# Output projection taken third by third, with all eight weight pieces resident and each third's norm behind its last step

## The reference

```python
def merge_and_mlp(h, ret_o, fox_o, ga, gb, w_ret_out, w_fox_out, w_o, norm2_g, w_ff1, w_ff2):
    m = jax.nn.sigmoid(ga) * (ret_o @ w_ret_out) + jax.nn.sigmoid(gb) * (fox_o @ w_fox_out)
    h = h + m @ w_o
    u = jax.nn.relu(rmsnorm(h, norm2_g) @ w_ff1)
    return h + (u * u) @ w_ff2
```

## Time and profile before

| what | us |
|---|---|
| median of 3 runs | 2191.03 |
| lowest and highest of them | 2190.86, 2191.83 |
| the profiled execution, its own time | 2192.57 |
| its span, first to last instruction | 2190.9 |
| PE busy in it | 2140.1 (98%) |
| DVE busy | 1066.9 (49%) |
| ACT busy | 543.5 (25%) |
| mean granted clock of TensorE | 0.995 of full speed |

### The profile page before, as it was taken

The page is one execution under the profiler, slowest core; times in us unless marked ns, Lnnn a source line. Parts: engine busy times, 40 slices in busy tenths (PEclk is TensorE's granted clock), DMA queues, the critical chain, the costliest instruction groups (busy, mean ns, idle before and its releaser), DMA issues.

```text
span 2190.9 us, 31673 instructions
## 1 busy us (share of the span) xinstructions
PE 2140.1 (98%) x12659; PEld 2002.2 (91%) x12659; DVE 1066.9 (49%) x2183; ACT 543.5 (25%) x1108; POOL 49.9 (2%) x93
## 2 busy tenths in 40 slices
PE   5999999999999999999999999999999999999998
PEld 4878888889998899989989999999999999999998
DVE  5354522256666666665665635574333333333333
ACT  4423200022222222221132323231212212122130
POOL 0000000000000000000000000000000000000000
PEclk9999999999999999999999999999999999999999
DMA  4222232433232333246434542012111111111111
GB/s 140 81 81 79 79 119 79 143 113 99 87 120 68 124 123 104 90 133 220 134 120 149 172 149 68 20 39 65 42 49 48 39 49 48 47 41 48 49 39 80
DMA packets 186189, 195.93 MB, mean 89 GB/s; under 512 B 9480, under 2 KB 156616, under 8 KB 186064
## 3 DMA queue, kind: packets, MB, share of 16 engines
q1 hardware_dynamic: 173904, 149.37, 22.3%
q0 software_dynamic: 12160, 44.72, 5.4%
HBM read 145.02 MB, written 49.04 MB: 89 GB/s over the span
## 4 chain that ended last, share of the span: by engine, by line
PE 92%; DVE 4%; issue 1%; ACT 1%; DMA 1%; DVEq 0%; SPq 0%; ACTq 0%
PE ps_mlp L303 37%; PE ps_dense L303 24%; PE ps_dense L324 18%; PE ps_out L928 4%; PE ps_scores L897 3%; PE ps_turn L881 2%; DVE w_lo L290 1%; PE ps_scores L973 1%; PE ps_turn L874 1%; PE ps_scores L979 1%; PE ps_scores L978 1%; DVE act_lo L364 0%; PE ps_turn L879 0%; DVE hn_T L1783 0%; PE ps_turn L1010 0%
## 5 line engine op out<-in xcount | busy, mean ns | idle before, releaser
L303 PE MATMUL ps_dense<-act_hi,w_lo 128*128 128x352 f32 (+2 forms) x1152 | 386.6, 336 | 0.6 <-DVE gated L1648 0.6
L303 PE MATMUL ps_dense<-act_hi,w_hi 128*128 128x352 f32 (+2 forms) x1152 | 384.8, 334 | 0.0
L303 PE MATMUL ps_dense<-act_lo,w_hi 128*128 128x352 f32 (+2 forms) x1152 | 384.7, 334 | 0.0
L303 PE MATMUL ps_mlp<-act_hi,w_lo 128*128 128x352 f32 x960 | 312.7, 326 | 3.5 <-DVE act_lo L1775 3.4
L303 PE MATMUL ps_mlp<-act_lo,w_hi 128*128 128x352 f32 x960 | 310.5, 323 | 0.0
L303 PE MATMUL ps_mlp<-act_hi,w_hi 128*128 128x352 f32 x960 | 310.1, 323 | 0.0
L279 ACT CAST w_hi<-w_raw 128x1024 fp32r<-128x1024 f32 x132 | 137.4, 1045 | 458.0 <-PE ps_mlp L303 283.8
L303 PE MATMUL ps_mlp<-u_lo,w_hi 128*128 128x352 f32 x768 | 248.0, 323 | 0.0
L303 PE MATMUL ps_mlp<-u_hi,w_lo 128*128 128x352 f32 x768 | 247.7, 323 | 0.0
L303 PE MATMUL ps_mlp<-u_hi,w_hi 128*128 128x352 f32 x768 | 247.6, 322 | 0.0
L303 PEld LDWEIGHTS ps_dense<-act_hi,w_hi 128*128 128x128 f32 x1152 | 218.0, 189 | 4.8 <-issue 1.6
(11 more groups left out here) (256 smaller groups left out, 2952.8 us busy)
## 6 DMA issues: line engine op xcount, KB each, us to landing
w_raw<-in_w_in SPq DMA_DIRECT2D x65, 512.0 KB, 4.3
w_raw<-in_w_ff SPq DMA_DIRECT2D x64, 512.0 KB, 3.9
gates<-stage POOLq DMA_DIRECT2D x24, 528.0 KB, 3.8
stage<-gates SPq DMA_DIRECT2D x16, 528.0 KB, 3.7
negc_rows<-neg_cumsum SPq DMA_DIRECT2D x8, 792.0 KB, 7.5
rotated<-stage POOLq DMA_DIRECT2D x8, 536.0 KB, 3.0
fox_out_T<-fox_stage POOLq DMA_DIRECT2D x8, 528.0 KB, 4.7
ret_gate_T<-gates SPq DMA_DIRECT2D x8, 528.0 KB, 4.8
```

Of the source, the lines that this page charges most:

```text
L303: mm = nc.tensor.matmul(bank(n)[:, 0:w], lhs[:, k, m0:m0 + P], rhs[:, k, c:c + w], start=(x == 0), stop=(x == 3 * kc - 1))
```

## The change

The steps of the output projection now go third by third throughout: all eight pieces for third 0 (steps 0 to 7), then for third 1 (8 to 15), then for third 2 (16 to 23). For that all eight pieces stay resident. Pieces 0 to 3 keep the four slots; pieces 4 to 7 lie in two new tiles `w_o_hi` and `w_o_lo`, which take the memory of `merged_T` once it has been split into `act_hi` and `act_lo` (ACT waits for that with `act.wait_ge(a_lo, A_M)`). `hn_T` moves to another place. The six remaining weight splits move: pieces 2 and 3 stand around the split of the merged rows' last third, pieces 4 to 7 in iterations 0 to 3, and the first four pieces of the MLP in iterations 18 to 21. `sum_third` of third 0 and 1 stand behind steps 10 and 18, their roots in iterations 11 and 19, and their norms in iterations 12 to 15 and 20 to 23, two chunks in each. The last `h_sum(23)` stands behind the loop. The norm of third 2 moves one MLP step ahead.

```diff
@@ arenas @@
-    _, rt, _, hsq = arena([("to_roots", [P, 19040], F32), ("roots", [P, 6, 352], F32), ("sums_kept", [P, TOUT], F32),
-                           ("h_squares", [P, 2, 352], F32)])
+    _, rt, _, hsq, hnt = arena([("to_roots", [P, 19040], F32), ("roots", [P, 6, 352], F32), ("sums_kept", [P, TOUT], F32),
+                           ("h_squares", [P, 2, 352], F32), ("hn_T", [P, 2, 352], F32)])
+    _, woh, wol = arena([("stage_kept4", [P, 2, TALL], F32), ("w_o_hi", [P, 4, UNIT], F32R), ("w_o_lo", [P, 4, UNIT], F32R)])
@@ ring @@
+        if U_WO + 4 <= u.first < U_MLP:
+            return u.first - U_WO + 2
@@ order @@
-    WO_STEPS = [(q, j) for q in range(4) for j in range(3)] + [(q, j) for j in range(3) for q in range(4, KC)]
+    WO_STEPS = [(q, j) for j in range(3) for q in range(KC)]
@@ tensor @@
-            pe.wait_ge(n2_add, 4 * j + 13)
+            pe.wait_ge(n2_add, 7 * j + 7)
-            turned_step(pe, At(N_WO + i), (U_WO + q) % 4, c, w)
-            if i in (16, 22):
-                sum_third((i - 16) // 6)
+            turned_step(pe, At(N_WO + i), ring(At(U_WO + q)), c, w)
+            if i in (10, 18):
+                sum_third((i - 10) // 8)
@@ scalar @@
             act.wait_ge(m_ok, 3 * KC - 2 + j)
+            if j == 2:
+                split_hi(act, At(U_WO + 2), At(N_WO - 3))
             resplit_hi(j, m_rows)
-            if i >= 5:
-                act.wait_ge(n2_add, i - 4)
+            if i >= 2:
+                wait(act, n2_add, i - 2 - (i - 2) // KC)
-        split_hi(act, At(U_WO + 2), At(N_WO - 3))
         split_hi(act, At(U_WO + 3), At(N_WO))
+        act.wait_ge(a_lo, A_M)
         for i in range(24):
-            if i in (3, 6, 9, 12):
-                split_hi(act, At(U_WO + i // 3 + 3), At(N_WO + i))
-            if i in (21, 22):
-                split_hi(act, At(U_MLP + i - 21), At(N_WO + i))
+            if i < 4:
+                split_hi(act, At(U_WO + 4 + i), At(N_WO))
+            if 18 <= i < 22:
+                split_hi(act, At(U_MLP + i - 18), At(N_WO + i - 1))
             h_square(i)
-            if i in (16, 22):
-                h_root((i - 16) // 6)
-            if i in (17, 18):
-                h_hi(0, range(4 * i - 68, 4 * i - 64))
+            if i in (11, 19):
+                h_root((i - 11) // 8)
+            if i >= 12 and i % 8 >= 4:
+                h_hi((i - 12) // 8, range(2 * (i % 4), 2 * (i % 4) + 2))
-        for q in range(2):
-            split_hi(act, At(U_MLP + q + 2), At(N_MLP + q - 1))
-        h_hi(1, range(KC))
         h_root(2)
-            if s in (1, 2):
-                h_hi(2, range(4 * s - 4, 4 * s))
+            if s in (0, 1):
+                h_hi(2, range(4 * s, 4 * s + 4))
@@ vector @@
-            wait(dve, n2_add, i - 3)
+            wait(dve, n2_add, i - 1 - i // KC)
+        split_lo(dve, At(U_WO + 2))
         resplit_lo(dve, 2, m_rows, A_RET)
-        split_lo(dve, At(U_WO + 2))
+        split_lo(dve, At(U_WO + 3))
         for i in range(24):
+            if i < 4:
+                split_lo(dve, At(U_WO + 4 + i))
+            if 18 <= i < 22:
+                split_lo(dve, At(U_MLP + i - 18))
             h_read(i)
-            if i and i not in (16, 20):
+            if i:
                 h_sum(i - 1)
-            if i in (15, 19, 23):
-                h_sum(i)
-            if i in (0, 3, 6, 9, 12):
-                split_lo(dve, At(U_WO + i // 3 + 3))
-            if i in (21, 22):
-                split_lo(dve, At(U_MLP + i - 21))
-            if i in (16, 22):
-                h_scale((i - 16) // 6)
-            if i in (17, 18):
-                h_norm(0, range(4 * i - 68, 4 * i - 64))
+            if i in (11, 19):
+                h_scale((i - 11) // 8)
+            if i >= 12 and i % 8 >= 4:
+                h_norm((i - 12) // 8, range(2 * (i % 4), 2 * (i % 4) + 2))
+        h_sum(23)
-        for q in range(2):
-            split_lo(dve, At(U_MLP + q + 2))
-        h_norm(1, range(KC))
         h_scale(2)
-            if s in (1, 2):
-                h_norm(2, range(4 * s - 4, 4 * s))
+            if s in (0, 1):
+                h_norm(2, range(4 * s, 4 * s + 4))
```

More of the change, by code:

```diff
@@ L164, in hybrid_step @@
     xrow = xrow[:, 0:2 * D].rearrange("p (b d) -> p b d", b=2)
-    _, rt, _, hsq = arena([("to_roots", [P, 19040], F32), ("roots", [P, 6, 352], F32), ("sums_kept", [P, TOUT], F32),
-                           ("h_squares", [P, 2, 352], F32)])
+    _, rt, _, hsq, hnt = arena([("to_roots", [P, 19040], F32), ("roots", [P, 6, 352], F32), ("sums_kept", [P, TOUT], F32),
+                           ("h_squares", [P, 2, 352], F32), ("hn_T", [P, 2, 352], F32)])
+    _, woh, wol = arena([("stage_kept4", [P, 2, TALL], F32), ("w_o_hi", [P, 4, UNIT], F32R), ("w_o_lo", [P, 4, UNIT], F32R)])
     _, yout = arena([("to_y_rows", [P, 19040], F32), ("y_rows", [P, 2, D], F32)])
-    uh, ul, relu, usq, hnt = arena([
-        ("u_hi", [P, 4, TOUT], F32R), ("u_lo", [P, 4, TOUT], F32R), ("relu", [P, 2, 352], F32), ("u", [P, 2, 352], F32),
-        ("hn_T", [P, 2, 352], F32)])
+    uh, ul, relu, usq = arena([
+        ("u_hi", [P, 4, TOUT], F32R), ("u_lo", [P, 4, TOUT], F32R), ("relu", [P, 2, 352], F32), ("u", [P, 2, 352], F32)])
     pt = ctx.enter_context(nc.psum_tensor("ps_turn", [P, 2, 512], F32))
@@ L260, in ring @@
             return (0, 2, 3, 1, 4, 5)[u.first % 6]
+        if U_WO + 4 <= u.first < U_MLP:
+            return u.first - U_WO + 2
         return 1 + (u.first - U_TURN) % 3 if u.first < U_GB else u.mod(4)
     def slot_hi(x):
-        return wh[:, x, :] if x < 4 else wxh[:, x - 4, :]
+        return wh[:, x, :] if x < 4 else (wxh[:, x - 4, :] if x < 6 else woh[:, x - 6, :])
     def slot_lo(x):
-        return wl[:, x, :] if x < 4 else wxl[:, x - 4, :]
+        return wl[:, x, :] if x < 4 else (wxl[:, x - 4, :] if x < 6 else wol[:, x - 6, :])
     def load_unit(sp, u, src):
```

## The result

| | median us | lowest, highest | runs |
|---|---|---|---|
| before | 2191.14 | 2189.73, 2192.01 | 16 |
| after | 2186.08 | 2184.64, 2187.37 | 16 |

The ratio is 0.9977, 95% interval 0.9970 to 0.9984: 5.1 us or 0.23% faster (by the interval 0.16 to 0.30%). The forecast was 2185.8. The fastest run before (2189.73) is slower than the slowest after (2187.37), but each kernel spreads over 2 to 3 us, more than the three runs known at first had shown.

The account below looks back on a forecast made before the run. PE, busy 98% of the span, was taken to bound the kernel. Two waits gone (-5.56 us) and a new one (+0.25) gave -5.3 us, from the median 2191.03 to 2185.8 us, range 2184.5 to 2188.6.

Parts of the forecast that it names:

- What bounds: PE, busy for 98% of the span; what it wins ahead of 1465 us shifts all behind one for one.
- The two waits: PE's waits for the norms of thirds 1 and 2: 0.28 + 5.28 us, 1.67 of it half speed, all gone.
- The steps: Output projection's 24 steps in the new order: its end stays at 1429.8 us, worth 0.
- Eight pieces in eight steps: Output projection's weight pieces, one per step of third 0: all in time, tightest by 1.4 us, cost 0.
- Rival C: Weight pieces can't keep pace in the projection's first eight steps: 2191 to 2197 us; chance 0.04.
- Norm of third 1, norm of third 2: DVE's norms ready earlier: third 1 10 us before need, third 2 at about 1454.9, 7 us to spare.
- The new wait: PE waits 0.25 us at the sum of third 2 for DVE's last square sum; bounds 0 and 1.5.
- Rival B: PE's wait at the sum of third 2 is 1.2 to 1.5 us: 2186.6 to 2186.9 us; chance 0.18.
- Rival A: The 1.67 us of half speed behind PE's wait isn't in every execution: gain 3.6 us, 2187.4; chance 0.13.
- The sum: Whole kernel: -5.56 + 0.25 = -5.3 us, against the median of 2191.03 this makes 2185.8 us.

Follow-up runs that it names:

- e10_order_and_sum: New order and resident pieces, norms and MLP splits where the kernel before has them, but sum and roots of third 1 behind step 18; 2192.03 us, ratio 1.0005.
- e3_two_numbers: Kernel before, in its own order, with sum and roots of third 1 behind step 20 in place of 22; 2191.30 us, ratio 1.0004.
- e4_wait_2us: Changed kernel with norm of third 2 one MLP step later and three extra reciprocals on DVE, results unused; 2189.21 us.
- e8: Kernel before, with sum and roots of third 1 behind step 21 in place of 22, norm of third 2 one MLP step earlier; 2189.47 us, ratio 0.9993.
- e2: Changed kernel's order and resident pieces, with sums, roots, norms and MLP splits where the kernel before has them; 2191.89 us, ratio 1.0005.
- e9: Changed kernel with four extra reciprocals on DVE ahead of the split of weight piece 5, results unused; 2190.59 us.
- e5: Changed kernel with norm of third 2 one MLP step later and four extra reciprocals on DVE, results unused; 2191.63 us.
- a0_after: Changed kernel run again unaltered, as yardstick for one set of runs; 2185.57 us, ratio 0.9978.
- a1_after: Changed kernel run again unaltered, as yardstick for another set of runs; 2185.75 us, ratio 0.9977.

## Why the prediction was right

*What bounds.* Right. PE's row to the end shifted one for one: behind its last long row the kernel before has 2190.9 - 1465.18 - 688.35 = 37.4 us, the changed one 2184.0 - 1435.61 - 711.08 = 37.3, so nothing was given back.

*The two waits, 5.56 us.* Right, and gone in the trace. The step that a reader could have doubted, 1.67 us of half speed as part of the wait's price, is shown by the two runs with the wait put back: 2.2 us of wait cost 3.8, 3.7 us cost 6.5. Shown is that such a part belongs to the price, not its size: it was 1.7 us in one and 2.8 in the other, and how it falls for a given wait no run lets me foretell.

*The steps, at 0.* A small miss: steps took 3.864 to 3.873 us where 3.847 was assumed, 0.4 us in all. So the new order is not quite worth 0: 0.3 of this lies in the 24 steps of the projection, and every trace of the new order shows it (last section).

*Eight pieces in eight steps, at 0.* Right. Piece 3 had its low part at 1344.3 against a need at 1345.6, 1.3 us early (forecast: 1.4), pieces 5 to 7 some 2.7 to 3.4. Rival C is out: PE began to wait only when 9.6 us of work stood ahead of piece 5's subtraction, and the delay didn't add up over the two buffers. That every landing is slow, as in the rival, was not tried.

*Norm of third 1, norm of third 2.* Right in time: third 2 was ready at 1453.3, with the due time at 1459.8, 6.6 us early (forecast: 7). But I had told the reason too simply, as DVE being late with roots and norms. Three runs say that early roots alone bring nothing that can be measured: in the old order because the sum then waits for DVE (3.2 us), or the MLP's splits for their loads (2.2 us); in the new order because of those loads alone (5.4 us). In the changed kernel the four splits stand in iterations 18 to 21, so that the loads run beside the roots and norms of third 1. They can stand there because in the new order the four slots are last read in steps 16 to 19; in the old one in 20 to 23. So the new order gives two things: third 1 is complete after step 15, so that the early sum finds its squares (no wait in e10_order_and_sum, 3.2 us in e3_two_numbers), and the slots are free four steps earlier. The first is shown not to be enough. That the second makes the difference is argued from the code and the traces, as no run moves the splits alone. Which of the remaining three edits (splits early, norm of third 1 interleaved, norm of third 2 a step earlier) would do without the others was not tried.

*The new wait, 0.25.* Right in place and cause, 0.40 in the traces of the changed kernel; moving one operation takes it away. Rival B (1.2 to 1.5) is out.

*Rival A (the clock fall isn't in every execution).* The price holds in the medians, so it isn't what decided here. Its core is not refuted, though: in e10_order_and_sum PE stood 2.6 us for third 1 and kept its clock, while 2.2 us in e4_wait_2us lost it. The windows of e10_order_and_sum, at this stand and at the second one, of 3.6 us, which lost it as before:

```profile
1443.00:1445.80 2.80, 0.34 (x3) 1.00 0.00 0
1445.80:1449.50 3.70, 3.69 (x23) 1.00 0.00 0
1461.20:1464.90 3.70, 0.26 (x3) 1.00 0.01 2
1465.40:1468.90 3.50, 3.50 (x14) 0.51 0.00 0
```

*The sum.* -5.3 forecast, -4.8 in the stage by the traces, -5.1 by the medians. What is missing is 0.4 of pace and 0.15 at the sum. The measured 0.23% lies above the 0.2% that I had set as the measurable change, but the interval begins at 0.16%, so that it is beyond 0.2% is not shown. That the medians come within 0.3 us of the forecast is partly luck: it was reckoned from three runs (2191.03), and the medians of before since then go from 2190.4 to 2191.1.

## What to carry to other kernels

A wait of the bounding engine is priced by the matmul that would have been due, counted past the slow stretch behind it, not by its length in the view of waits: here 5.3 us for a wait that the view lists with 3.4. That price is the one of the trace at hand: the half clock behind a stand came out at 1.7 or 2.8 us, and once at nothing. An operation that is moved earlier takes its cover with it: the roots had hidden two weight loads, and without them the engine stood for the loads. And a new order of work is best judged by what it lets others do earlier, here a sum without a wait and slots that are free sooner: the order by itself gave nothing.

## What the runs showed of the hardware that was not expected

**Whether the clock falls doesn't go by the length of the stand alone.** Stands of 2.2 (e4), 2.4 (e8), 3.4 (e3), 3.5 (e2), 3.6 (before, and the second one in e10) and 3.9 us (e9) brought 3.4 us each at 0.50 of the clock (1.2 in place of 2.4 GHz). One of 3.7 us (e5) brought 6.8 us, of which 1.0 lay in the stand itself. One of 2.6 us (the first in e10) brought none, nor did 1.3 us in e3_two_numbers. When it falls varies too: 1.2 us after PE had resumed in e4, 1.4 in e9, 0.2 in the kernel before, and during the stand in e3, e5 and e8. This fits what the Trainium skill says in "TensorE: Matmul & The Clock Gate", Part 1, that activity is judged in windows that run freely and don't begin with the kernel's own events.

**The same kernel meets other falls in other executions.** Two traces of the changed kernel, the first one and a0_after, over the same stretch of an earlier stage:

```profile
1101.00:1105.00 4.00, 3.73 (x13) 0.57 1.03 357
1101.00:1105.00 4.00, 3.86 (x21) 1.00 0.95 328
```

And near 150 us the clock is down for 3.4 us in these two, for 6.8 in a1_after. Part of the spread of the times goes with this: of the 108 executions of the kernel before, the 45 with a mean clock of 0.997 have a mean span of 2188.2 us, the 21 with 0.995 or less one of 2189.8. So rival A describes something that happens in this kernel; but the three traces that have the wait in its old place and length (before, e2_order_alone, e10_order_and_sum) all have the fall behind it.

**The pace of matmuls varies at full clock.** A step of 24 matmuls takes 3.84 us in some stretches and 3.88 in others, that is 160.0 or 161.7 ns a matmul on average (single distances go from 155 to 167). In the projection all eleven traces of the new order have the slow pace from step 4 to 19 (in e9_piece_late_4 not in the two steps behind its slow stretch); the three of the old order have 3.84 to 3.86 up to step 19, but for the sum. In the long stretch of the MLP the traces of both kernels agree step by step: twelve steps with two of three at 3.88, then twelve with two of three at 3.85. In the first steps of the MLP even traces of the same kernel differ (a0_after and a1_after). What sets the pace stays open.
